# Routing from the centred stream in a hybrid decoder step, and five changes of order

## What is computed

```python
x = layer_norm(ALPHA * x + mix, ln1_w[layer], ln1_b[layer])
ff = moe(x, router_w, router_bias, w_gate[layer], w_up[layer], w_down[layer])
x = layer_norm(ALPHA * x + ff, ln2_w[layer], ln2_b[layer])

def layer_norm(x, w, b):
    mu = x.mean(-1, keepdims=True)
    var = jnp.square(x - mu).mean(-1, keepdims=True)
    return (x - mu) * lax.rsqrt(var + EPS) * w + b

def moe(t, ...):                       # t is the normed stream
    scores = sigmoid(t @ router_w)
    sel = scores + router_bias         # the best group of four, its top two experts
    ...
    y = sum over e of gates[:, e] * ((silu(t @ w_gate[e]) * (t @ w_up[e])) @ w_down[e])
```

## Time and profile before

| | |
|---|---|
| timed executions | 1019.34, 1019.91, 1023.15 us |
| profiled execution | 1023.78 us, span 1021.7 us, mean granted clock 0.985 |
| busy share of the span | PE 95%, PEld 61%, DVE 37%, ACT 27%, POOL 10% |
| chain that ended last | PE 78%, DMA 9%, DVE 7%, ACT 3%, issue 2% |
| GLA and SSD stages, layer 0 | to about 239 us |
| output projection and first norm, layer 0 | 239 to 307 us |
| router, routing, gather, layer 0 | 307 to 330 us |
| experts, layer 0 | 330 to 554 us |
| layer 1: mixer, norm, router, experts | to 750, 757, 781, 1005 us |
| transfers | 299.63 MB, DMA share near 1 during most of the expert loops |

### The profile page before, as it was taken

One profiled execution on the slowest core, in us unless ns is written; L12 is line 12 of the kernel. 1 busy time (PEld: TensorE's weight loads), 2 busy tenths in 40 slices (PEclk: granted clock), 3 DMA queues, 4 the chain that ended last, 5 costly groups with the idle time before them and its releaser, 6 DMA issues.

```text
span 1021.7 us, 12645 instructions
## 1 busy us (share of the span) xinstructions
PE 971.2 (95%) x4959; PEld 626.4 (61%) x4959; DVE 377.8 (37%) x931; ACT 273.4 (27%) x589; POOL 100.3 (10%) x167
## 2 busy tenths in 40 slices
PE   8989999889997999999998899999989999999996
PEld 6767777667876454544535787777866354545434
DVE  2457786844015121211114336665134021212114
ACT  3534434122014100000002247887132100100002
POOL 2321223251000000000000000113100000000000
PEclk9999999999999999999999999999999999999999
DMA  9943535966832899999999534442782999999991
GB/s 381 349 170 130 190 151 190 372 256 243 344 112 94 362 422 413 420 421 421 421 421 427 211 133 151 168 153 88 310 348 91 424 413 422 422 420 421 421 380 44
DMA packets 38990, 299.63 MB, mean 293 GB/s; under 512 B 4808, under 2 KB 6344, under 8 KB 8456
## 3 DMA queue, kind: packets, MB, share of 16 engines
q1 hardware_dynamic: 33696, 268.52, 64.7%
q0 software_dynamic: 4544, 29.65, 7.8%
q10 hardware_dynamic: 688, 0.60, 0.2%
HBM read 283.32 MB, written 15.53 MB: 292 GB/s over the span
## 4 chain that ended last, share of the span: by engine, by line
PE 78%; DMA 9%; DVE 7%; ACT 3%; issue 2%; POOL 0%; ACTq 0%; DVEq 0%; POOLq 0%
PE bank L1193 20%; PE bank L1217 10%; PE bank L1353 7%; PE bank L839 7%; PE bank L1086 6%; PE bank L1228 5%; PE bank L1178 5%; DMA ring<-in_w_up 4%; PE bank L1340 4%; PE bank L1107 2%; PE bank L1121 2%; PE bank L1115 1%; DMA spread<-v_rows 1%; DMA W<-in_conv_cols 1%; DMA spread<-xd_rows 1%
## 5 line engine op out<-in xcount | busy, mean ns | idle before, releaser
L1193 PE MATMUL bank<-ring,A 128*64 128x512 f32 x880 | 223.0, 592 | 2.4 <-issue 1.7
L839 PE MATMUL bank<-xT,ring 128*128 128x264 f32 x704 | 165.4, 391 | 4.0 <-ACT A L1438 2.6
L839 PEld LDWEIGHTS bank<-xT,ring 128*128 128x128 f32 x704 | 132.2, 191 | 34.3 <-issue 10.7
L1193 PEld LDWEIGHTS bank<-ring,A 128*64 128x64 f32 x880 | 73.8, 137 | 124.1 <-issue 124.1
L1217 PE MATMUL bank<-ring,W 128*64 128x512 f32 x448 | 113.4, 595 | 0.9 <-ACT W L1671 0.9
L2241 DVE TENSOR_TENSOR W<-W,bank 128x512 f32<-128x512 f32 x16 | 11.0, 687 | 204.5 <-PE bank L1193 204.5
L1353 PE MATMUL bank<-xT,ring 128*128 128x264 f32 x320 | 78.9, 395 | 0.0
L1217 PEld LDWEIGHTS bank<-ring,W 128*64 128x64 f32 x448 | 34.9, 137 | 60.9 <-issue 59.8
L1353 PEld LDWEIGHTS bank<-xT,ring 128*128 128x128 f32 x320 | 58.8, 192 | 11.4 <-issue 1.8
L764 POOL TENSOR_SCALAR xT<-xT,vecs 128x264 f32<-128x264 f32 x4 | 5.6, 1399 | 604.3 <-DVE xT L2095 604.3
L1193 PE MATMUL bank<-A 128*64 128x512 f32 x144 | 63.5, 592 | 0.8 <-DMA ring<-in_w_up 0.8
(11 more groups left out here) (313 smaller groups left out, 1142.7 us busy)
## 6 DMA issues: line engine op xcount, KB each, us to landing
ring<-in_w_gate SPq DMA_DIRECT2D x56, 1024.0 KB, 13.8
ring<-in_w_down SPq DMA_DIRECT2D x56, 1024.0 KB, 13.7
ring<-in_w_up SPq DMA_DIRECT2D x54, 1024.0 KB, 16.9
ring<-in_w_ab SPq DMA_DIRECT2D x10, 2048.0 KB, 8.5
ring<-in_w_c SPq DMA_DIRECT2D x8, 2048.0 KB, 13.9
A<-in_w_up SPq DMA_DIRECT2D x10, 1024.0 KB, 14.0
ring<-in_w_oab SPq DMA_DIRECT2D x4, 2048.0 KB, 11.0
A<-in_w_gate SPq DMA_DIRECT2D x8, 1024.0 KB, 13.1
```

The costliest lines, as they stand in the source:

```text
L839: mm = pe.matmul(ab_bank(m)[:, 0:T], slot(AB_IN0 + m // 4, 8)[:, c, (m % 4) * P:(m % 4 + 1) * P], xT[:, c, :], start=(c == 0), stop=(c == ...
L1193: mm = pe.matmul(bank[i][64 * j:64 * j + 64, :], xg[:, 2 * (pair % 2) + j, c, :], slot(n0 + 6 * pair + 2 * i + j, 8)[:, c, :], start=(c == ...
```

## The change

- The router no longer waits for the normed stream. `fold_router` (DVE, ahead of `add_out`) multiplies the router's weights by `ln1_w` and sums them with `ln1_b` to a bias row. PE's router matmuls read the centred chunks, directly behind the sum of squares. DVE multiplies the result by `lnr` (`rooted_logits`), and the bias row comes in as a second matmul in each of the three last router steps.
- PE also turns `lnr` into a column; ACT scales the token rows by it as it copies them. What is gathered is then norm without weight and bias, and these are applied where the gathered parts are copied out of PSUM: two affine steps of 224 columns in place of one copy of 448 (`gathered`).
- The scaling and the bias adds of the stream itself (`norm_scale`, `norm_add`) come behind the routing on DVE, and between the gathered parts on ACT; POOL's copies of the decode tokens and ACT's residual copy wait for them.
- Order 1: in the last GLA head, the last two `conv_tanh` come ahead of the second `take_ab` of its late part.
- Order 2: in the first GLA head, four of the eight decays come behind the projection copy.
- Order 3: in layer 1, `copy_k(0)` comes ahead of the exponentials of head 1.
- Order 4: in the SSD stage, the score product comes ahead of `decode_states(0)`.
- Order 5: in layer 0, PE's `norm_squares(1)` comes ahead of the overflow code, inside `If(flag < 1)`; the overflow code has its own copy of it.

The diff, cut to its core (the second of each pair of calls for layer 1 is like the first):

```diff
@@ -277,12 +277,15 @@
-        def gathered(eng, copy, i, g):
+        def gathered(eng, affine, i, g):
...
             eng.wait_ge(sem("gather_ready"), 4 * g + (i + 1))
-            copy(xg.rearrange("p e c s -> p c e s")[:, 2 * i:2 * i + 2, :, 0:PCAP],
-                 gather_bank(i)[:, 0:8 * PCAP].rearrange("p (c e s) -> p c e s", c=2, e=4)).then_inc(
-                sem(f"xg_copied{i % 2}"), 1)
+            for c in (2 * i, 2 * i + 1):
+                at = 8 * (g // GATHERS) + c
+                done = affine(xg[:, :, c, 0:PCAP],
+                              gather_bank(i)[:, c % 2 * 4 * PCAP:(c % 2 + 1) * 4 * PCAP].rearrange("p (e s) -> p e s", e=4),
+                              cols[:, V_LN1W + at:V_LN1W + at + 1], cols[:, V_LN1B + at:V_LN1B + at + 1])
+            done.then_inc(sem(f"xg_copied{i % 2}"), 1)
@@ -752,6 +758,8 @@
+                for c in range(DC):
+                    normed_chunk(pool, 2 * layer, c)
@@ -766,8 +774,8 @@
             stage_end(pool, 2)
+            stage_end(pool, 3)
             norm_adds(0, V_LN1B)
-            stage_end(pool, 3)
@@ -1125,11 +1133,14 @@
                 for c in range(DC):
-                    normed_chunk(pe, 2 * layer, c)
                     q = c % 4
-                    mm = pe.matmul(bank[2][32 * q:32 * q + 32, 0:T], router[:, c, :], xT[:, c, :],
+                    mm = pe.matmul(bank[2][32 * q:32 * q + 32, 0:T], folded[:, c, :], xT[:, c, :],
...
                 mm.then_inc(sem("moe_logits"), 1)
+                pe.wait_ge(sem("norm_roots"), 2 * layer + 1)
+                for b in range(2):
+                    tr = pe.transpose(bank[3][:, P * (b + 1):P * (b + 2)], lnr[:, b * P:(b + 1) * P], ident[:, :])
+                tr.then_inc(sem("xtm_turned"), 1)
@@ -1142,8 +1153,10 @@
                 for b, n in enumerate((P, P, NB)):
-                    mm = pe.matmul(bank[2][0:n, 288 + 16 * b:304 + 16 * b], logits4[:, b * P:b * P + n], quarter[:, :],
-                                   start=True, stop=True)
+                    pe.matmul(bank[2][0:n, 288 + 16 * b:304 + 16 * b], logits4[:, b * P:b * P + n], quarter[:, :],
+                              start=True, stop=False)
+                    mm = pe.matmul(bank[2][0:n, 288 + 16 * b:304 + 16 * b], ones[:, 0:n], folded_bias[:, 0:E_N],
+                                   start=False, stop=True)
@@ -1269,7 +1282,14 @@
+                return flag
+
+            def over_experts(layer, flag):
+                E0 = E_N * layer
...
                 with pe.If(flag > 0):
+                    for c in range(DC):
+                        normed_chunk(pe, 2 * layer, c)
@@ -1302,14 +1322,24 @@
                     mm.then_inc(sem("over_resummed"), 1)
-                return flag
-
-            def settle_over(flag):
-
-                with pe.If(flag < 1):
-                    for name, k in (("gates", 1), ("sel", E_N), ("gu", 4 * E_N), ("down", DC * E_N), ("read", E_N),
-                                    ("resummed", 1)):
-                        pe.sem_inc(sem("over_" + name), k)
+                    if layer == 0:
+                        norm_squares(1)
+
+            def settle_over():
+
+                for name, k in (("gates", 1), ("sel", E_N), ("gu", 4 * E_N), ("down", DC * E_N), ("read", E_N),
+                                ("resummed", 1)):
+                    pe.sem_inc(sem("over_" + name), k)
+
+            def finish_experts(layer, flag):
+
+                if layer == 0:
+                    with pe.If(flag < 1):
+                        norm_squares(1)
+                        settle_over()
+                over_experts(layer, flag)
+                if layer == 1:
+                    norm_squares(3)
@@ -1324,8 +1354,7 @@
             over_flag = experts(MOE0, 0)
-            norm_squares(1)
-            settle_over(over_flag)
+            finish_experts(0, over_flag)
@@ -1452,8 +1481,10 @@
                 for m in range(AB_POINTS[3 * h + 2], AB_POINTS[3 * h + 3]):
+                    if h == 3 and m == AB_POINTS[3 * h + 2] + 1:
+                        conv_tanh(TANH_AT[h, 2])
                     take_ab(m)
-                    if m == AB_POINTS[3 * h + 3] - 1:
+                    if h < 3 and m == AB_POINTS[3 * h + 3] - 1:
@@ -1517,24 +1548,27 @@
-                def decay_states(h):
+                def decay_states(h, b0=0, b1=NB):
...
                             slot_ready(act, (HG_ST0 if layer else GLA_ST0) + i)
-                    for b in range(NB):
+                    for b in range(b0, b1):
...
                         mul = act.activation(s, s, ACT.Copy, scale=decx[:, h, b:b + 1])
-                    mul.then_inc(sem("heads_decayed"), 1)
+                    if b1 == NB:
+                        mul.then_inc(sem("heads_decayed"), 1)
...
                     copy_v(0)
+                    copy_k(0)
...
                 between()
-                copy_k(0)
+                if layer == 0:
+                    copy_k(0)
@@ -1547,10 +1581,15 @@
                         exps(layer, h + 2)
-                    if h + 1 < nh:
-                        decay_states(h + 1)
                     late = late_fill(h)
-                    next(late)
+                    if layer == 0 and h == 0:
+                        decay_states(1, 0, 4)
+                        next(late)
+                        decay_states(1, 4, NB)
+                    else:
+                        if h + 1 < nh:
+                            decay_states(h + 1)
+                        next(late)
@@ -1612,6 +1651,12 @@
+            def norm_add(k, bcol, c):
+
+                act.wait_ge(sem("norm_scaled"), DC * k + c + 1)
+                act.activation(xT[:, c, :], xT[:, c, :], ACT.Identity, bias=cols[:, bcol + c:bcol + c + 1]
+                               ).then_inc(sem("norm_done_act"), 1)
@@ -1622,18 +1667,17 @@
                 act.activation(lnr[:, :], lnr[:, :], ACT.Exp, scale=-0.5).then_inc(sem("norm_roots"), 1)
+                if k % 2 == 0:
+                    act.preload_act_table_set(after)
+                    return
                 for c in NORM_ADDS["act"]:
-                    act.wait_ge(sem("norm_scaled"), DC * k + c + 1)
-                    act.activation(xT[:, c, :], xT[:, c, :], ACT.Identity, bias=cols[:, bcol + c:bcol + c + 1]
-                                   ).then_inc(sem("norm_done_act"), 1)
+                    norm_add(k, bcol, c)
...
                 E0 = E_N * layer
-                act.wait_ge(sem("moe_logits"), 3 * layer + 1)
-                act.copy(logits4, bank[2][:, 0:T]).then_inc(sem("moe_logits"), 1)
@@ -1641,12 +1685,24 @@
                 for i in range(4):
-                    act.wait_ge(sem("xtm_turned"), 4 * layer + i + 1)
-                    act.copy(xtm[:, i // 2, (i % 2) * 512:(i % 2 + 1) * 512], bank[4 + i][:, :]).then_inc(
-                        sem("xtm_copied"), 1)
+                    act.wait_ge(sem("xtm_turned"), 5 * layer + i + 2)
+                    if i == 0:
+                        act.wait_ge(sem("row_roots"), layer + 1)
+                    act.activation(xtm[:, i // 2, (i % 2) * 512:(i % 2 + 1) * 512], bank[4 + i][:, :], ACT.Copy,
+                                   scale=row_roots[:, i // 2:i // 2 + 1]).then_inc(sem("xtm_copied"), 1)
+
+                def affine(out, x, w, b):
+                    return act.activation(out, x, ACT.Identity, scale=w, bias=b)
+
+                gathered(act, affine, 0, GATHERS * layer)
+                for c in NORM_ADDS["act"][0:2]:
+                    norm_add(2 * layer, V_LN1B + 8 * layer, c)
+                gathered(act, affine, 2, GATHERS * layer)
+                for c in NORM_ADDS["act"][2:4]:
+                    norm_add(2 * layer, V_LN1B + 8 * layer, c)
+                for c in range(DC):
+                    normed_chunk(act, 2 * layer, c)
                 act.activation(xacc[:, :, :], xT[:, :, :], ACT.Copy, scale=ALPHA).then_inc(sem("moe_residual"), 1)
-                for i in (0, 2):
-                    gathered(act, act.copy, i, GATHERS * layer)
@@ -2031,12 +2087,12 @@
                     sums_read(0)
-                decode_states(0)
...
                     dve.sem_inc(sem("ssd_scores"), 1)
+                decode_states(0)
@@ -2084,12 +2140,34 @@
-            def layer_norm(k, src, wcol, bcol):
+            def layer_norm(k, src):
...
+
+            def fold_router(layer):
+
+                at = 8 * layer
+                st.run(dve.tensor_tensor(folded, router, cols[:, V_LN1B + at:V_LN1B + at + DC].rearrange(
+                    "p (c o) -> p c o", o=1).to_broadcast([P, DC, ROUTER_W]), ALU.mult))
+                st.run(dve.tensor_reduce(folded_bias, folded.rearrange("p c e -> p e c"), AX, ALU.add))
+                st.run(dve.tensor_tensor(folded, router, cols[:, V_LN1W + at:V_LN1W + at + DC].rearrange(
+                    "p (c o) -> p c o", o=1).to_broadcast([P, DC, ROUTER_W]), ALU.mult))
+
+            def rooted_logits(layer):
+
```

(23 more changed lines are left out.)

22 lines of the change are left out of this document (14 added, 8 removed).

## The result

| | before | changed |
|---|---|---|
| median | 1020.66 us (1019.34 to 1023.15) | 1007.28 us (1005.67 to 1011.93) |
| profiled execution | 1023.78 us | 1011.93 us |
| its span, mean granted clock | 1021.7 us, 0.985 | 1010.2 us, 0.985 |

The ratio is 0.988, with a 95% interval of 0.985 to 0.992: faster by 8 to 16 us. Of 21.1 us, 13.4 came in the medians and 11.5 between the two profiled spans.

What follows compares the result with a forecast made beforehand. TensorE, busy 95% of the span, was taken as the bound, so gains were its waits: 2.65 + 1.35 + 7.0 + 3.2 + 2.7 + 1.0 + 3.2 = 21.1 us off 1019.91, forecast 998.8, range 991 to 1007.

Steps and rivals of the forecast that it cites:

- three signs: Wrong if the updates' transfer lands unmoved, routing starts over 5.5 behind the squares, or expert loops show a new wait over 1 us.
- First head: First GLA head: four decays behind the projection's copy, 1.65 of wait plus 1.0 of clock; 2.65 us taken, bounds 1.6 and 2.7.
- Tanhs: Last GLA head: two convolution tanhs ahead of the second copy let it start 1.35 us earlier; bounds 0.6 and 1.35.
- SSD stage: Score product ahead of the first four state updates: 1.9 us in group 0, 7.0 taken for both, bounds 5.4 and 8.1.
- Router: Second norm to experts, both layers: routing starts 3.55 us earlier, part is given back behind the gather; 3.2 gained per layer.
- POOL may make its four copies, 0.77: Router passage behind the gather: after ACT's adds at 326.05, POOL copies in 0.77 us and releases the decode inputs at 327.0.
- first rival: Scaling behind the routing takes the router's place: each layer gains 0.5 us in place of 3.2; 1004.2 us, chance 0.12.
- without the fall of the clock in the gather: Router case: the gather is 2 us shorter, DVE and POOL are late at 325.8, gain 4.3 us in place of 3.2.
- Squares ahead of the jump: Layer 0, second norm: 4.1 us won less 1.4 for the branch's pause behind the squares; 2.7 taken, bounds 1.0 and 4.1.
- From the new place, 557.55: Squares term: 6.4 us of branch from 557.55 gives 563.9; the next projection could run from 562.5, so 1.4 lost.
- lower bound of 1.0: Squares term: worth only 1.0 us if the clock falls in the longer pause instead.
- Keys: Layer 1: key copy ahead of head 1's exponentials, against a PE wait of 1.9 us; 1.0 taken, bounds 0 and 1.9.

Runs made afterwards that it cites:

- The kernel with the gap filled: The changed kernel with 14 spare matmuls in place of 10 ahead of the counting of places, both layers; 1003.33 us, ratio 0.985.

## Why the forecast was off, step by step

None of the three signs that I had named for being wrong came: the updates' transfer landed 7.1 earlier, 1.7 more than the tanhs and the first head had moved it; the routing starts 3.4 behind the squares; no wait inside the expert loops is over 1 us. What failed lies in two places that I had not put under a sign, the copies on POOL and the place of the jump.

*First head.* The step was right (1.65 of order). The clock that came back was 1.75 and not 1.0, and the landing of that execution was 0.9 earlier, which is luck. *Tanhs.* Right: 1.35 forecast, 1.3 found in the pair of traces; no run takes this order back alone.

*SSD stage.* The mechanism was right: the updates end where I had put them, within 0.4 on the moved scale, and the transfer's landing moved with the kernel. The mis-sized term is what PE does then. I had it arrive with the updates; with the full clock under its score matmuls it arrives 2.1 before them, and in this execution it falls to half clock behind that wait: 5.3 in place of 7.0. Where the clock held, in nine of 15 profiles, the stage gave 6.3 to 7.1, as forecast.

*Router.* The front of the passage came out better than forecast: 16 matmuls took 1.10, not 2.0. The step that failed is "POOL may make its four copies, 0.77". I took the duration from a place where DVE was idle and used it where DVE multiplies, although my own count had DVE free for its products at 326.7, before the copies were done at 327.0. The copies took 3.04, and behind the wait of 3.7 the first expert matmuls took 1.7 more, a term that my sum didn't have. Net 0.6 and 0.75 in place of 3.2 twice. My first rival had this number (0.5 a layer) and the place, but let DVE's own list grow, which it didn't. Where the gap ahead of the places is filled, the timelines against the kernel before give 3.0 in layer 0 (with 1.7 lost to the clock under the experts) and 4.9 in layer 1, so 7.9: more than forecast, and near my 4.3 a layer "without the fall of the clock in the gather".

*Squares ahead of the jump.* The mechanism was right, its size was not. I had subtracted 1.4 for the pause at its new place. The step that failed is "From the new place, 557.55": that is where the means end. PE can reach the jump only when ACT has delivered the last square for it, at 560.7 on the same scale, and 6.4 from there is 567.1; the changed kernel went on at 568.0. The projection itself could run from 564.4 and not from 562.5, since the norm's own wait of 2.19 stands ahead of it. So the jump costs 3.5 there (5.72 against 2.19), and the projections begin at half clock. My lower bound of 1.0 named the second effect and was still too high: the pair of traces says -0.8, and none of the twelve profiles with the new order and the jump is better than the kernel before in this stretch. The rule that I cited for it (the Trainium skill, Runtime: NRT & Kernel Launch, Instruction fetch mechanics: a taken branch out of the window stalls for a fetch) is borne out by the kernel without the jump, 2.19 in place of 5.72.

*Keys.* I took the middle of 0 and 1.9 although I had named the wait that would take its place. It was 0: the waits of 1.70 and 1.16 for the projected chunks took back what came at the keys.

Together: 3.5 for the squares' place, 1.0 for the keys, 1.7 for the SSD stage, 5.05 for the two routers and 0.4 at the start are missing, and 2.0 came unasked; that is the 9.6 between 21.1 and 11.5. This is the account of one pair of executions, and 1.7 of it (the SSD stage) and most of the 5.05 are what the clock and the edge at the gather did in this one. By the medians 7.7 are missing. The kernel with the gap filled, in which no copy is slow, is at 1003.33, 4.5 above the forecast, which is about the squares' 3.5 and the keys' 1.0.

## What to carry to other kernels

A duration belongs to its neighbours: before an instruction is moved, look at what the neighbour will be doing at the new place (here VectorE beside GpSimd). A wait ahead of dense matmuls can have a second price, the clock that falls behind it in some executions (here 1.65 and 1.7, behind waits of 2.1 to 3.7 us); it belongs into the range. One profile is one execution: before a term is taken as measured, look for the same stretch in the other traces. And where two engines end within 1 us of each other ahead of such a wait, the kernel has two schedules; some spare matmuls, or 2 us less on the longer list, settle which one runs.

## What the runs showed of the hardware

Four copies on GpSimd of 128x64 took 0.77 us beside an idle VectorE or one that reads PSUM, and 2.97 to 3.04 where two of them met its products of two SBUF operands, 1.2 us each (1.76 where one did). A single copy took 0.24, or 1.2 to 1.4 beside a product, and ended 0.1 behind it. The other way round, a VectorE product of two SBUF operands, 0.42 us elsewhere, took 4.5 where GpSimd made four products of 1.05 each.

The profiled executions of the kernels with the router's new form show 28 waits of over 1 us ahead of the first expert matmul of a layer. Behind those of 1.2 to 1.5 us the clock fell under the 64 matmuls in none of 4 (13.95 us), behind those of 2.3 in 7 of 17 (15.5 to 15.7), behind those of 3.6 to 3.7 in 4 of 7 (15.65 and 16.9); so the length of the wait alone doesn't decide it, and what does is left open. A jump over a large body, taken while weights were on the queues, left TensorE idle for 5.5 to 6.3 us in all where it was 2.19 without the jump, with a packet of the instruction queue in each piece of the pause. The landing of one broadcast transfer in the first head moved by 2 us between executions of nearly the same program.
